# Convolution state of a hybrid decoder layer stored from its columns in four-byte pieces

## What is computed

```python
h = rmsnorm(x, attn_norm_w)
xin, bg, cg, q, k, v, g_conv, g_attn = split(h @ w_in)
u = cg * xin
conv_out = causal_depthwise_conv3(u, prefix)        # prefix: zeros (prompt), state_conv (sample)
conv_state = concat([prefix, u])[:, -2:]            # an output: last two gated inputs
y_conv = bg * conv_out
y_attn = window_attention(rmsnorm(q), rmsnorm(k), v)   # window 128, bias, sinks
x = x + (sigmoid(g_conv) * y_conv + sigmoid(g_attn) * y_attn) @ w_out
x = x + moe(rmsnorm(x))                              # top-4 of 32 experts, 12 MB of weights each
```

## Time and profile before

| | |
|---|---|
| median of 3 runs | 1182.07 us (1181.87 to 1182.19) |
| profiled execution: time / span | 1181.89 / 1180.0 us |
| PE busy | 1118.8 us, 95% |
| DVE, ACT, POOL busy | 35%, 16%, 1% |
| moved by DMA | 442.03 MB, 375 GB/s on average |
| chain that ended last | PE 59%, DMA 39% |

### The profile page before, as it was taken

How to read it: one execution, slowest core, us unless ns; L and a number is a source line. 1 busy time by engine, 2 the same in 40 slices (tenths; PEclk the granted TensorE clock), 3 DMA queues, 4 the chain that set the end, 5 groups by cost and what they waited for, 6 DMA issues and landing times.

```text
span 1180.0 us, 13885 instructions
## 1 busy us (share of the span) xinstructions
PE 1118.8 (95%) x5602; PEld 502.6 (43%) x5631; DVE 411.9 (35%) x838; ACT 191.4 (16%) x360; POOL 16.5 (1%) x31
## 2 busy tenths in 40 slices
PE   9999999999999999999989898989999999999997
PEld 5688888653333333333333333333333333333332
DVE  4754353664353323323131323232222323232322
ACT  2123313421131010101011111101010101010101
POOL 1100000000000000000000000000000000000000
PEclk9999999999999999999999999999999999999999
DMA  9945325839999999999999999999999999999995
GB/s 318 368 165 179 119 96 200 340 114 400 413 394 429 433 428 434 430 429 431 437 429 432 432 432 430 433 433 430 431 432 432 432 432 432 431 432 434 423 427 237
DMA packets 39278, 442.03 MB, mean 375 GB/s; under 512 B 3602, under 2 KB 8978, under 8 KB 23644
## 3 DMA queue, kind: packets, MB, share of 16 engines
q1 hardware_dynamic: 36776, 435.09, 88.0%
q0 software_dynamic: 1648, 5.83, 1.6%
q10 hardware_dynamic: 820, 0.62, 0.2%
HBM read 440.23 MB, written 2.36 MB: 375 GB/s over the span
## 4 chain that ended last, share of the span: by engine, by line
PE 59%; DMA 39%; issue 1%; DVE 0%; ACT 0%; ACTq 0%; SPq 0%
PE pA L1467 26%; PE pB L1467 24%; DMA ring<-in_w_up 18%; DMA ring<-in_w_down 12%; DMA area<-in_w_up 8%; PE pM L1467 7%; PE pM L1470 1%; PE pA L1470 1%; DMA x<-in_x_prompt 1%; ACT area L862 0%; SPq L553 0%; DVE conv_row L1245 0%; DVE x L1330 0%; ACT area L867 0%; ACTq L704 0%
## 5 line engine op out<-in xcount | busy, mean ns | idle before, releaser
L1467 PE MATMUL pA<-ring,hn 128*64 128x512 f32 x1536 | 352.9, 602 | 26.5 <-DMA ring<-in_w_up 26.4
L1467 PEld LDWEIGHTS pA<-ring,hn 128*64 128x64 f32 x1536 | 105.3, 137 | 222.4 <-issue 184.6
L1467 PE MATMUL pB<-area,ring 128*128 128x264 f32 (+1 forms) x928 | 184.4, 388 | 0.0
L1467 PE MATMUL pB<-ring,area 128*64 128x512 f32 (+1 forms) x768 | 166.8, 595 | 9.1 <-DMA ring<-in_w_down 7.8
L1467 PEld LDWEIGHTS pB<-area,ring 128*128 128x128 f32 (+1 forms) x928 | 143.7, 175 | 32.9 <-issue 2.6
L1467 PE MATMUL pA<-area,hn 128*64 128x512 f32 x512 | 119.4, 610 | 10.9 <-DMA area<-in_w_up 10.9
L1467 PEld LDWEIGHTS pB<-ring,area 128*64 128x64 f32 (+1 forms) x768 | 56.5, 135 | 101.7 <-issue 92.9
L1330 DVE TENSOR_TENSOR x<-pM,x 128x512 f32<-128x512 f32 x64 | 42.8, 691 | 150.3 <-PE pM L1467 150.2
L850 ACT ACTIVATE area<-area 128x512 f32<-128x512 f32 x30 | 18.9, 630 | 396.1 <-DVE area L1313 396.1
L1245 DVE COPY conv_row<-pM 128x512 f32<-128x512 f32 x30 | 20.6, 686 | 155.2 <-PE pM L1467 155.2
L1467 PEld LDWEIGHTS pA<-area,hn 128*64 128x64 f32 x512 | 36.0, 139 | 75.1 <-issue 59.1
(11 more groups left out here) (274 smaller groups left out, 781.2 us busy)
## 6 DMA issues: line engine op xcount, KB each, us to landing
ring<-in_w_up SPq DMA_DIRECT2D x36, 4096.0 KB, 29.8
ring<-in_w_down SPq DMA_DIRECT2D x18, 4096.0 KB, 29.4
ring<-in_w_up SPq DMA_DIRECT2D x24, 2048.0 KB, 12.9
area<-in_w_up SPq DMA_DIRECT2D x12, 4096.0 KB, 30.2
area<-in_w_down SPq DMA_DIRECT2D x6, 4096.0 KB, 30.1
ring<-in_w_in SPq DMA_DIRECT2D x22, 1024.0 KB, 12.5
ring<-in_w_down SPq DMA_DIRECT2D x10, 2048.0 KB, 10.5
area<-in_w_up SPq DMA_DIRECT2D x8, 2048.0 KB, 12.9
```

Of the source, the lines that this page charges most:

```text
L1467: return pe.matmul(out, w, m, start=start, stop=stop, skip_group_check=True)
```

## The change

The transposes, copies and bank uses of `conv_rows` go. POOL stores, for each of the eight column tiles, two columns and eight columns of `cx` straight into the two outputs. In HBM the features run fastest and in `cx` they run over the partitions, so every number is a piece of 4 bytes by itself: 256 and 1024 pieces a tile. The stores stand in POOL's queue where the two had stood, the first four tiles behind `XIN_END[0]`, the others behind `XIN_END[1]`. They have a semaphore of their own, `conv_stored`; SP waits for all sixteen before j = 10, in place of the wait for `conv_rows`. `stored` counts six instead of eight.

```diff
-    after[34].append(("conv_rows", 0))
-    after[36].append(("conv_rows", 1))
...
                 if j == 10:
                     sp.wait_ge(misc_free, FILL["values", 3])
-                    sp.wait_ge(misc_free, FILL["conv_rows", 1])
+                    sp.wait_ge(conv_stored, 16 * 2 * KT)
                     sp.wait_ge(bias_loaded[0], 48)
                     sp.wait_ge(bias_loaded[1], 48)
...
             load_table(4)
-            pool.wait_ge(misc_free, FILL["conv_rows", 1])
-            pool.dma_start(conv_prompt[0, 0], conv_row[0:2, :]).then_inc(stored, 16)
-            pool.dma_start(conv_sample[0, :, 1, :], conv_row[2:2 + DEC, :]).then_inc(stored, 16)
+            for t in range(KT):
+                pool.wait_ge(tile_free_dve, DVE_TILES[XIN_END[t // 4]])
+                f = slice(128 * t, 128 * t + 128)
+                pool.dma_start(conv_prompt[0, 0, :, f].rearrange("j p -> p j"), cx[:, t, SEQ:SEQ + 2],
+                               allow_slow_non_contiguous=True).then_inc(conv_stored, 16)
+                pool.dma_start(conv_sample[0, :, 1, f].rearrange("b p -> p b"), cx[:, t, SEQ + 2:],
+                               allow_slow_non_contiguous=True).then_inc(conv_stored, 16)
...
-            pool.wait_ge(stored, 16 * 8)
+            pool.wait_ge(stored, 16 * 6)
...
-                            act.wait_ge(stored, 16 * 8)
+                            act.wait_ge(stored, 16 * 6)
...
-                elif what == "conv_rows":
-                    b = misc_bank()
-                    V.tensor_copy(conv_row[0:2 + DEC, 512 * a:512 * a + 512], b[0:2 + DEC, :]).then_inc(misc_free, 1)
...
-                    dve.wait_ge(stored, 16 * 8)
+                    dve.wait_ge(stored, 16 * 6)
...
-                elif what == "conv_rows":
-                    b = misc_bank()
-                    pe.wait_ge(tile_free_dve, DVE_TILES[XIN_END[a]])
-                    for t in range(4):
-                        mm = tr(b[0:2 + DEC, 128 * t:128 * t + 128], cx[:, 4 * a + t, SEQ:])
-                    mm.then_inc(misc_full, 1)
```

More of the change, by code:

```diff
@@ L487, in build @@
         stored = sem("stored")
+        conv_stored = sem("conv_stored")
         final_stored = sem("final_stored")
```

## The result

The changed kernel takes 1223.41 us (median of six executions, 1215.86 to 1239.06) against 1182.12 before. Two of the six (1234.42 and 1239.06) are slow ones, over 1.5% above the fastest; the other four have a median of 1221.89, 39.8 us over before, and the ratio of 1.0326 (95% interval 1.0312 to 1.034) is theirs. Forecast was 1181.3, in a range up to 1184.4.

The account below looks back on a forecast made before the run. The expert-weight stream runs at the DMA's rate, its start set by TensorE's chain before 250 us. Chain -0.77, everything else 0, from 1181.89 gives 1181.1; with 0.18 for the median, 1181.3 us, range 1179.8 to 1184.4.

Parts of the forecast that it names:

- The start of the stream at 250 us: Expert load j = 4 at 250.09 us waits for TensorE; time gained before it should reach the end undiminished.
- Transposes: Two groups of four leave TensorE's chain, between scores and tiles and between tiles: 0.33 + 0.44 = 0.77 us gained.
- Copies: Two VectorE copies of 0.68 us go; TensorE waits for neither, so they were valued at nothing.
- removed waits: VectorE and ScalarE wait for six stores instead of eight; both waits come over 15 us later: nothing.
- GpSimd's issue time: Issuing the sixteen stores on GpSimd: 6.6 us a group, hidden, with 26.5 us to spare before the bias loads.
- disturbance while the stores are issued: Rival: GpSimd's issues hold up VectorE's bank releases, so TensorE waits some 3 us; 1184.5 us or more, chance 0.05.
- One sign: Sign of being right: in TensorE's chain, tile pieces run from scores at 164.1 us or so without transposes.
- What a piece costs on the DMA engines: Cost of each 4-byte store piece: 13 to 122 ns on an engine, lower end taken; even 122 ns called hidden.
- slow pieces: Rival: small HBM writes exceed the bounds, delaying bias loads, then SP's expert loads; some 1242 us at 244 ns, chance 0.10.
- Nothing: Cost to SP's w_in and w_out loads of sharing DMA engines with the pieces: none; 4.2 us a group without cover.
- a delay D costs nothing ... up to 18.1 us: Late bias loads delay SP's expert loads from j = 10; hidden before j = 4 at 250.09 for D up to 18.1 us.
- The estimate by the Trainium skill: If each piece paid 0.2 us in turn, 640 pieces take 128 us, ending at 242.4; the kernel's end near 1214.

Follow-up runs that it names:

- the run with runs of columns: Changed kernel, its sixteen stores sent to an HBM scratch as pieces of 8 and 32 bytes, convolution state left out of the outputs: 1181.03 us, ratio 0.9988.
- the first group alone: Changed kernel with only the first four column tiles stored in 4-byte pieces, the others to an HBM scratch in 8- and 32-byte runs: 1188.46 us, ratio 1.0057.

## Why the prediction was wrong

**Right.** The start of the stream at 250 us sets the end, to within 2.9 us: +54.4 there is +57.3 at the end, and in the run with runs of columns -0.96 there (249.13 against 250.09) is -1.0 in the span (1179.0 against 1180.0). Transposes: 0.77 worked out, 0.78 in the trace of the changed kernel. Copies, removed waits and GpSimd's issue time (6.4 us a group against 6.6) came as forecast. VectorE's products beside the issues, at 118.38 and 177.37 us, take 0.43 us as before, so the rival "disturbance while the stores are issued" did not happen. One sign was misread: by the prediction's own rows the tiles start behind the scores at 162.89 + 1.93 = 164.82 and not at 164.1; 164.65 was measured in the run with runs of columns.

**The step that failed** is "What a piece costs on the DMA engines". It took 13 ns a piece on each engine from a load into SBUF, called 122 ns an upper bound from the same load, and built the sum, the range and the 0.10 for slow pieces on the two. In the loop a piece side by side with its neighbours cost 166 ns (rows 4 KB apart; the changed kernel's 8 KB was not tried side by side there), with its neighbours 64 bytes away 7 ns. Both ends came from rows of another operation: loads of 128 and 512 bytes with landing places of their own. A bound from all the latency of such a load says nothing of writes that lie side by side. With it fell the "Nothing" for the loads that share the DMA engines with the pieces: the first group alone, with no bias load near, cost 7.2 us.

**A second step failed beside it:** "a delay D costs nothing ... up to 18.1 us". It followed SP's queue and the stream only. The bias landing had two more waiters, ScalarE's cast and, behind it in ScalarE's own order, the gate tiles that free TensorE's banks. ScalarE in the kernel before:

```profile
198.14 0.39 ACT L760 ACTIVATE tmp<-pB 128x264 f32<-128x264 f32 x1 [3.17 <-PE pB L1467]
198.42 1.90 ACT L786 ACTIVATE keys<-area 96x2048 bf16<-96x2048 f32 x1
201.70 0.39 ACT L760 ACTIVATE tmp<-pB 128x264 f32<-128x264 f32 x1 [1.37 <-PE pB L1467]
...
205.26 0.39 ACT L760 ACTIVATE tmp<-pB 128x264 f32<-128x264 f32 x1 [2.23 <-PE pB L1467]
```

TensorE has two banks and fills one in 3.56 us; the one ready at 201.70 it wants back at 205.26. By then ScalarE must have done the cast and the copy behind it, 1.90 and 0.39 us, so an estimate from these rows leaves the cast some 4.5 us. A delay of 5.9 us, the forecast's own for 122 ns, would have reached TensorE by a little over 1 us: the claim that even 122 ns would be hidden was wrong on its own terms, if by little. With the bias landing 57 us later, the same wait cost TensorE 25.3 us. What stands queued behind a waiting instruction had been followed on GpSimd and SP and not on ScalarE.

**Of the rivals,** slow pieces was the right one, at 0.10, and its price by the upper estimate (244 ns, 1242 us) stood nearer to the truth than the forecast. That was luck in part. SP did wait for the bias loads, for 64.6 us, but not for the reason given, biases behind stores in GpSimd's queue: from a queue without stores they took about as long (23.0 us to landing), and 6 of the 41 us come with no 4-byte store right ahead of the biases. The estimate by the Trainium skill ("DMA: Bandwidth & Descriptors", Specifications and Latency and other measured facts: read-modify-write below 512 bytes, 0.2 us for an HBM access on average) gave 1214, near 1223, but not for a reason that the runs bear out: pieces of 4 bytes in stretches of 512 bytes of their own, or 64 bytes apart, are just as much below 512 bytes; the first cost nothing in the projection stage, the second nothing there and 7 ns each in the loop.

## What to carry to other kernels

Price a store by the addresses it writes, not by its bytes or its number of pieces: pieces of 4 bytes side by side in HBM cut the rate of the weight stream from 431 to 111 GB/s and made the bias loads of GpSimd's and of ScalarE's queue late, while the same pieces in SBUF or 64 bytes apart in HBM passed unnoticed in the projection stage (the latter cost 4.8 us in the loop). When no row of the trace shows an operation, bounds from another operation's rows are not bounds; keep real weight on the other side, or weigh it first where there is no slack. And ask of every landing who waits for it on each engine, with what is queued behind that wait.

## What the hardware showed that was not expected

- The price of a 4-byte write into HBM spans 7 to 166 ns a piece and engine in this stream, by layout alone.
- While such writes drain, DMA engines count as busy (0.96) at a quarter of their rate (111 of 431 GB/s), with the weights' own packets taking 4.00 us in place of 1.08.
- In the changed kernel VectorE and ScalarE stop with their inputs ready, VectorE for 7.7 us (129.6 to 137.27), ScalarE for some 9 (197.2 to 206.25), and TensorE for up to 5.93 us in the midst of a tile.
- TensorE's granted clock falls with these stalls: 0.83 on average from 130 to 160 us, where it was 1.00. The tile that follows the stop of 3.03 us took 5.62 us, where four tiles in a row took 14.44 in this place before, 3.61 each; 1.00 is the 2.4 GHz level, and the average of 0.63 in the loop lies between it and the 1.2 GHz level (0.5).
- The loss is not in proportion: the first group of stores cost 7 us, both together 42 (each with the gained 0.8). The second group meets the bias loads, for which SP and ScalarE wait, so this says nothing of how the jam itself grows.
